# Head pairs in sparse and dilated attention, sums of 128 columns, and head gains folded into tables and copies

## The reference, cut to what matters

```python
# hybrid layer: native sparse attention, 4 heads of 64, for each of 4 blocks of 128 rows
kc, vc = compress_blocks(k, ...), compress_blocks(v, ...)        # 31 compressed keys
o_cmp = softmax(q kc^T/8 - slope*dist, causal) @ vc
o_sel = softmax over the selected blocks (all 8 blocks here, causal) @ v_s
o_win = softmax over the last 256 positions @ v_w
o = g0*o_cmp + g1*o_sel + g2*o_win

# conditioned layer l = 0, 1
qa, ka = rope(rms_norm(qa, gain_a[0])), rope(rms_norm(ka, gain_a[1]))   # 16 heads of 64 each
oa = diff_attention(qa, ka, va, lam)                                    # full 512 x 512
qb, kb = rope(rms_norm(qb, gain_b[0])), rope(rms_norm(kb, gain_b[1]))   # 12 heads of 64 each
# dilated windows (128,1), (512,4), (2048,16), 4 heads each, joined by their log-sum-exp
def rms_norm(x, g): return x * rsqrt(mean(x*x, -1) + EPS) * g
def apply_rope(x, cos, sin):            # rotates elements 0..7 with 8..15 of each 64
    x1, x2, rest = x[..., :8], x[..., 8:16], x[..., 16:]
    return concat([x1*cos - x2*sin, x2*cos + x1*sin, rest])
```

## Time and profile before

| | us |
|---|---|
| median of 3 runs | 3395.01 (3390.1 to 3413.55) |
| the profiled execution | 3409.53 |
| its span | 3407.3 |
| TensorE busy in it | 2996.8 (88%) |
| mean granted clock of TensorE | 0.872 |

### The profile page before, as it was taken

One profiled execution on the slowest core, in us unless ns is written; L12 is line 12 of the kernel. 1 busy time (PEld: TensorE's weight loads), 2 busy tenths in 40 slices (PEclk: granted clock), 3 DMA queues, 4 the chain that ended last, 5 costly groups with the idle time before them and its releaser, 6 DMA issues. The chain is left out here.

```text
span 3407.3 us, 35905 instructions
## 1 busy us (share of the span) xinstructions
PE 2996.8 (88%) x13881; PEld 2368.2 (70%) x13881; DVE 1712.8 (50%) x3234; ACT 1032.0 (30%) x2010; POOL 19.3 (1%) x58
## 2 busy tenths in 40 slices
PE   6969468886899679989999899998998999989999
PEld 5856357776688557657777688885766777768887
DVE  4223455555666365674233466645576424344444
ACT  2213221111422243543332322224354333332221
POOL 0000100000000000000000000000000000000000
PEclk8975567777899879989589899998998959999999
DMA  3210000000666202102023255521210202312221
GB/s 125 88 17 1 11 9 1 1 1 1 191 200 201 82 25 75 50 13 72 21 61 94 94 194 189 178 82 54 83 38 13 72 21 61 114 64 87 97 99 50
DMA packets 211058, 249.41 MB, mean 73 GB/s; under 512 B 12143, under 2 KB 124746, under 8 KB 210890
## 3 DMA queue, kind: packets, MB, share of 16 engines
q1 hardware_dynamic: 177056, 193.30, 17.7%
q10 hardware_dynamic: 33834, 53.83, 4.8%
HBM read 243.70 MB, written 2.10 MB: 72 GB/s over the span
## 5 line engine op out<-in xcount | busy, mean ns | idle before, releaser
L1863 ACT ACTIVATE weights_hi<-weight_ring 128x512 fp32r<-128x512 f32 (+1 forms) x240 | 143.9, 602 | 436.4 <-PE bank L1904 408.5
L1880 DVE TENSOR_TENSOR weights_lo<-weight_ring,weights_hi 128x512 fp32r<-128x512 f32 (+1 forms) x240 | 156.2, 654 | 235.6 <-ACT weights_hi L1863 235.6
L1904 PE MATMUL bank<-h_hi,weights_hi 128*128 128x512 f32 x512 | 209.7, 410 | 15.8 <-DVE h_lo L1880 9.5
L2676 PE MATMUL bank<-h_hi,weights_hi 128*128 128x512 f32 x512 | 204.0, 398 | 19.4 <-DVE h_lo L340 19.4
L789 PE MATMUL bank<-arena 64*128 64x512 f32 (+4 forms) x544 | 205.1, 614 | 17.4 <-PEq L972 11.0
L2596 ACT ACTIVATE weights_hi<-weight_ring 128x1024 fp32r<-128x1024 f32 x128 | 135.2, 1056 | 265.4 <-PE bank L2676 264.6
L2163 PE MATMUL bank<-chunk_hi,h_hi 128*128 128x512 f32 x448 | 185.5, 414 | 30.4 <-DVE h_lo L340 26.0
L1904 PE MATMUL bank<-h_lo,weights_hi 128*128 128x512 f32 x512 | 203.9, 398 | 0.0
L2676 PE MATMUL bank<-h_lo,weights_hi 128*128 128x512 f32 x512 | 203.8, 398 | 0.0
L2676 PE MATMUL bank<-h_hi,weights_lo 128*128 128x512 f32 x512 | 202.0, 395 | 0.0
L1904 PE MATMUL bank<-h_hi,weights_lo 128*128 128x512 f32 x512 | 201.8, 394 | 0.0
(11 more groups left out here) (442 smaller groups left out, 5892.8 us busy)
## 6 DMA issues: line engine op xcount, KB each, us to landing
arena<-in_ada_w ACTq DMA_DIRECT2D x48, 1024.0 KB, 5.4
weight_ring<-in_w_in SPq DMA_DIRECT2D x21, 2048.0 KB, 7.7
weight_ring<-in_w_in SPq DMA_DIRECT2D x65, 512.0 KB, 5.3
weight_ring<-in_w_mlp_up SPq DMA_DIRECT2D x16, 2048.0 KB, 8.2
weight_ring<-in_w_mlp_down SPq DMA_DIRECT2D x16, 2048.0 KB, 8.1
weight_ring<-in_w_out SPq DMA_DIRECT2D x6, 2048.0 KB, 7.9
weight_ring<-in_w_in SPq DMA_DIRECT2D x10, 1024.0 KB, 6.8
weight_ring<-in_w_branch_a SPq DMA_DIRECT2D x16, 512.0 KB, 6.4
```

Of the source, the lines that this page charges most:

```text
L1863: act.activation(hi, src, ACT.Copy).then_inc(*hi_done.one())
L1880: dve.tensor_tensor(lo, src, hi.bitcast(F32), ALU.subtract).then_inc(*lo_done.one())
L1904: ins = pe.matmul(out, ws[a_][:, n % PIECES, k - k0, :], tile["x"][b_][:, k, :], start=k + a_ + b_ == 0, stop=last[n] and k == k1 - 1 and ...
L2676: ins = pe.matmul(self.bank[t % NB][:], ws[a_][:, t % 2, k, :], x[b_][:, k, :], start=k + a_ + b_ == 0, stop=k == ND - 1 and a_ == 1)
```

## The change

1. In `attention` with one part in a unit (`nsa`, `dil`), TensorE takes the units by twos: the scores of two heads, then the transposes of the two before them, then the sums of the two before those. The row buffers are four, not three; `finish` runs six steps late, not four.
2. A sum in these stages has 128 columns of values, its head's 64 and the next 64. The columns too many are overwritten by the next head's sum. The last head of a `dil` group and the sums over compressed values stay at 64.
3. In `queries_keys` the product with the head gain is gone. For the 16 rotated elements of a head the gain is in tables of cos*gain and sin*gain; for the others it is a scale by row in ScalarE's copy from the bank, one copy for each of the four blocks. The four products of 64 columns become two of 128 (four of 64 in the chunk with queries and keys).
4. `layer_tables` loads the gains by row as well (8 more small loads of 64 rows x 2) and makes the tables (16 products of 64 columns, two memsets, two small products).

```diff
@@ attention
-        NROW = 3 * parts
+        by_twos = parts == 1
+        NROW = 4 if by_twos else 3 * parts
@@ tensor
+                def scores_of_two(n):
+                    two = units[n]["parts"] + units[n + 1]["parts"]
+                    if n >= S_BANKS:
+                        pe.wait_ge(*sig.maxima.at(n - S_BANKS + 2))
+                    lo, last = 0, len(two[0]["scores"]) - 1
+                    for j in range(last + 1):
+                        m = two[0]["scores"][j][1].shape[-1]
+                        for q, part in enumerate(two):
+                            lhsT, rhs = part["scores"][j]
+                            ins = pe.matmul(self.bank[(n + q) % S_BANKS][:, lo:lo + m], lhsT, rhs, start=True, stop=True)
+                            if j == last:
+                                ins.then_inc(*sig.scores.one())
+                        lo += m
-                steps((0, scores), (2, turn), (3, sums))
+                if by_twos:
+                    for n in range(0, N + 4, 2):
+                        if n < N:
+                            scores_of_two(n)
+                        for lag, run in ((2, turn), (4, sums)):
+                            if 0 <= n - lag < N:
+                                run(n - lag, units[n - lag])
+                                run(n - lag + 1, units[n - lag + 1])
+                else:
+                    steps((0, scores), (2, turn), (3, sums))
@@ vector
-                steps((0, maxima), (1, mix), (4, finish))
+                steps((0, maxima), (1, mix), (6 if by_twos else 4, finish))
@@ sparse_attention
-                        values = [self.ns[:, b, vcol:vcol + E] for b in range(b0, i + 1)]
+                        values = [self.ns[:, b, vcol:vcol + 2 * E] for b in range(b0, i + 1)]
@@ dilated
-                units.append(dict(parts=[part], group=2 * i, cols=(h * E, (h + 1) * E),
-                                  values=[vn[:, b, h * E:(h + 1) * E] for b in range(b0, b1)]))
+                more = E if h < H - 1 else 0
+                units.append(dict(parts=[part], group=2 * i, cols=(h * E, (h + 1) * E + more),
+                                  values=[vn[:, b, h * E:(h + 1) * E + more] for b in range(b0, b1)]))
@@ layer_tables, scalar
+                for l in range(2):
+                    for kind, name in enumerate(("qk_gain_a_2", "qk_gain_b_2")):
+                        for half in range(2):
+                            act.dma_start(self.row_gain[half * E:(half + 1) * E, l, kind, :],
+                                          a[name][l].rearrange("a e -> e a"), allow_slow_non_contiguous=True)\
+                               .then_inc(*landed.dma())
@@ layer_tables, vector
-                dve.wait_ge(*landed.all_of_stage(16 * 9))
+                dve.wait_ge(*landed.all_of_stage(16 * 17))
+                for l in range(2):
+                    for kind, gains in enumerate((self.gain_a, self.gain_b)):
+                        for j in range(2):
+                            tables = self.turns[:, l, kind, j, :].rearrange("p (i t a r) -> p i t a r", i=NT, t=2, a=2)
+                            by = gains[:, l, j, 0:2 * R].rearrange("p (a r) -> p a r", a=2).unsqueeze(1)\
+                                .broadcast_to([P, NT, 2, R])
+                            for t, angle in enumerate((self.cos, self.sin)):
+                                dve.tensor_tensor(tables[:, :, t], angle.unsqueeze(2).broadcast_to([P, NT, 2, R]), by,
+                                                  ALU.mult).then_inc(*self.dve_order.one())
@@ queries_keys, scalar
-                    act.activation(out, src, ACT.Copy).then_inc(*emptied.one())
+                    for j, which in enumerate(chunks[c][1]):
+                        to, from_ = out[:, j], src[:, j]
...
+                        ins = act.activation(to, from_, ACT.Identity, scale=self.row_gain[:, l, kind, which:which + 1])
@@ queries_keys, vector
-                    seq(tt(halves, halves, gains.unsqueeze(2).broadcast_to(shape), ALU.mult))
...
-                    for t, u, v in ((t1, x1, cos), (t2, x2, sin), (t3, x2, cos), (t4, x1, sin)):
-                        tt(t, u, v, ALU.mult).then_inc(*self.dve_order.one())
+                    for first in range(0, G, G // halves):
...
+                        for t, dst in enumerate((by_cos, by_sin)):
+                            tt(dst[:, gs], pairs[:, gs], tables[:, t].unsqueeze(1).broadcast_to([P, G // halves, 2, R]),
+                               ALU.mult).then_inc(*self.dve_order.one())
```

More of the change, by code:

```diff
@@ L755, in attention @@
         row_max = self.row_max
-        NROW = 3 * parts
+        by_twos = parts == 1
+        assert not by_twos or N % 2 == 0
+        NROW = 4 if by_twos else 3 * parts
         rows = self.take(NROW, T)
@@ L1027, in sparse_attention @@
                         part = dict(scores=[(qs[h], keys)], n=nk, table=table)
-                        values = [self.ns[:, b, vcol:vcol + E] for b in range(b0, i + 1)]
-                    units.append(dict(parts=[part], values=values, cols=(h * E, (h + 1) * E), group=g))
+                        values = [self.ns[:, b, vcol:vcol + 2 * E] for b in range(b0, i + 1)]
+                    units.append(dict(parts=[part], values=values, group=g,
+                                      cols=(h * E, h * E + values[0].shape[-1])))
                     if kind == 0:
@@ L2002, in layer_tables @@
         self.gain_a, self.gain_b = self.take(2, 2, E), self.take(2, 2, E)
+        self.turns = self.take(2, 2, 2, NT * 4 * R)
+        self.row_gain = self.take(2, 2, 2)
         self.subln = self.take(2, P)
@@ L2092, in _ @@
                     seq(ts_(self.gain_a[:, l, 0, :], self.gain_a[:, l, 0, :], E ** -0.5, None, ALU.mult))
+                    seq(ts_(self.row_gain[:, l, 0, 0:1], self.row_gain[:, l, 0, 0:1], E ** -0.5, None, ALU.mult))
                     seq(ts_(self.subln[:, l, :], self.subln[:, l, :], 1.0 - LAM[l], None, ALU.mult))
+                for half in range(2):
+                    dve.memset(self.row_gain[half * E:half * E + 2 * R], 1.0).then_inc(*self.dve_order.one())
+                dve.wait_ge(*self.act_ready.after("sin"))
+                for l in range(2):
[7 more added lines that the diff above has]
+                                                  ALU.mult).then_inc(*self.dve_order.one())
+                dve.wait_ge(*self.dve_order.all())
                 dve.wait_ge(*self.pool_ready.after("places"))
@@ L2131, in queries_keys @@
         R = E // 4 // 2
-        raw, sq = self.take(3, width), self.take(2, width)
+        raw, sq = self.take(3, width), self.obT
         ss = self.take(3, G)
-        t1, t2, t3, t4 = (self.take(G, R) for _ in range(4))
+        by_cos, by_sin = (self.take(G, 2, R) for _ in range(2))
         units = [(c, i) for c in range(len(chunks)) for i in range(NT)]
@@ L2202, in empty @@
                     src = self.bank[4 + n % 2][:, 0:width].rearrange("p (j t) -> p j t", j=NC_)
-                    if len(out.shape) == 4:
-                        src = src.rearrange("p j (b m) -> p j b m", b=NT)
-                    act.activation(out, src, ACT.Copy).then_inc(*emptied.one())
+                    for j, which in enumerate(chunks[c][1]):
+                        to, from_ = out[:, j], src[:, j]
+                        if len(to.shape) == 3:
+                            from_ = from_.rearrange("p (b m) -> p b m", b=NT)
+                        ins = act.activation(to, from_, ACT.Identity, scale=self.row_gain[:, l, kind, which:which + 1])
+                        if j < NC_ - 1:
+                            ins.then_inc(*self.x_landed.one())
+                    ins.then_inc(*emptied.one())
                 def split(n, c, i):
@@ L2232, in scale @@
                     seq(tt(x, x, ss[:, n % 3, :].unsqueeze(2).broadcast_to([P, G, E]), ALU.mult))
[L2233 to L2241 removed]
+                    pairs = x[:, :, 0:2 * R].rearrange("p g (a r) -> p g a r", a=2)
+                    halves = len(set(chunks[c][1]))
+                    for first in range(0, G, G // halves):
+                        gs = slice(first, first + G // halves)
+                        tables = self.turns[:, l, kind, chunks[c][1][first * E // P], :]\
+                            .rearrange("p (i t a r) -> p i t a r", i=NT, t=2, a=2)[:, i]
+                        for t, dst in enumerate((by_cos, by_sin)):
+                            tt(dst[:, gs], pairs[:, gs], tables[:, t].unsqueeze(1).broadcast_to([P, G // halves, 2, R]),
+                               ALU.mult).then_inc(*self.dve_order.one())
                     dve.wait_ge(*self.dve_order.all())
[L2243 removed]
+                    tt(pairs[:, :, 0, :], by_cos[:, :, 0, :], by_sin[:, :, 1, :], ALU.subtract)\
+                        .then_inc(*self.dve_order.one())
                     dve.wait_ge(*self.dve_order.all())
[L2245 removed]
+                    tt(pairs[:, :, 1, :], by_cos[:, :, 1, :], by_sin[:, :, 0, :], ALU.add).then_inc(*normed.one())
```

(8 more changed lines are left out.)

21 lines of the change are left out of this document (4 added, 17 removed).

## The result

The kernel after takes 3262.74 us (median of 4 runs, 3258.2 to 3270.46), the kernel before, beside it, 3396.56 (3390.1 to 3413.55): a ratio of 0.960, 95% interval 0.957 to 0.963. The forecast was 3268. The two profiled executions are 3409.53 and 3262.91 us long, 146.6 apart; the medians are 133.8 apart, since the profiled execution of before lies above its median.

What follows compares the result with a forecast made beforehand. TensorE, busy 88% of the span, was taken as the bound, at half clock in nsa and dil. Savings of 45 + 41 + 42 + 6.4 - 7 = 127.4 us gave 3395 - 127 = 3268, range 3240 to 3290.

Steps and rivals of the forecast that it cites:

- (a): Rival: clock stays at 1.2 GHz for its own reason, leaving only the paired scores' 65 us: 3331 us, chance 0.07.
- (b): Rival: clock stays low because transposes do not count as busy work: 3331 us, chance 0.05.
- (e): Rival: the halves do not run at once for two heads and the clock stays: 3396 us, chance 0.04.
- (d): Rival: slower, rounds run one behind the other because the second exponential is too late: 3459 us, chance 0.04.
- (c): Rival: clock rises late or falls back, above all in nsa, giving half its gain: 3300 us, chance 0.14.
- Stage by stage: Attention stages at full clock: dil 45 us instead of 86.4 and 87.0, nsa 72 instead of 117.5.
- the 12 us for the start at half clock: In nsa: it starts at half clock and its first twelve units hardly raise it, about 12 us more.
- the clock's paragraph: In nsa and both dil: rounds resembling the work before two earlier clock rises would lift the clock from about half.
- change 2's step: Sums of 128 columns in nsa and dil: cost taken as zero, at most 55 us; no gain except through the clock.
- The far rounds: Dil rounds of two far units: 2.2 us of TensorE; may lose 0.3 us each to ScalarE's queue, 7 us in all.
- Tables: Table stage: eight more loads delay VectorE's start by 3.9 us, plus products; 7 us more taken, loads' bounds 0 to 8.
- Head norms: The qk stages: middle hidden behind gapless TensorE projection, only the end shorter, 1.6 us in each of four, 6.4 saved.

Runs made afterwards that it cites:

- e6: The kernel after with 40 unused transposes in the table stage ahead of nsa: 3264.44 us against 3397.77 for the kernel before.
- x1: The kernel before with eleven unused transposes in dil's third and fourth step, where TensorE waits: 3333.3 us against 3394.06.
- x3: The kernel after with unused transposes in nsa's table stage, first two rounds and ahead of the first sixteen units' sums: 3261.0 us against 3394.06 before.
- e2: The kernel before with only the sums widened to 128 columns, one head at a time: 3363.48 us against 3408.62.
- e1: The kernel after with sums of 64 columns again, pairs of scores kept: 3287.87 us against 3408.62 for the kernel before.
- x8: The kernel after with sums of 64 columns and eleven unused transposes in dil's second and third round: 3274.94 us against 3399.37 before.
- x4: The kernel after with eleven unused transposes in dil's second and third round: 3265.15 us against 3394.06 for the kernel before.
- e7: The kernel after with ScalarE by twos, two exponentials and then two copies: 3263.52 us against 3397.77 for the kernel before.
- x5: The kernel after with the unused transposes of x3 and x4 and ScalarE's order of e7: 3257.8 us against 3394.06 for the kernel before.
- x7: The kernel before with x1's unused transposes in dil and more in nsa and its table stage: 3306.27 us against 3399.37.

## Why the prediction was right

**TensorE bounds the three stages; the clock rises.** Right: 0.96 and 1.00 in dil, and 1.00 in nsa from its 27th us on. Rivals (a), (b) and (e) fall with it, and (d) too: no round runs one behind the other. (c) had part of it, the late rise in nsa, but not its price. The rule behind (b), that the full clock does not engage for transposes, is in "TensorE: Matmul & The Clock Gate" of the Trainium skill, Part 4. The runs disagree: a transposes-only stretch at 1.00 (e6) and a stage that eleven transposes saved (x1).

**Stage by stage.** dil: 45 predicted, 43.9 and 42.6 measured; 41 and 42 saved predicted, 43.0 and 44.3 measured. nsa: 45 predicted, 48.8 measured. Of its terms, the 12 us for the start at half clock were too high: x3 takes it away and gains 1.5, at most 8.5 with the time of its own transposes taken off.

**What the clock's paragraph got wrong.** Its conclusion held and its reason only in part, so that it was partly luck. It compared what TensorE did before the two rises with dil0, and took the rounds of 64 rows and narrow sums as work under which the clock is low. It missed that 0.53 in the earlier trace rows is not 0.50: each dil stage began at full clock and lost it after about 5 us (0.03 x 2 x 87). The old rounds hold the clock for a whole stage when that wait is filled (x1: 52.5 us). What is poor in them is that they do not win it back, and neither do one-head rounds with wide sums (e2, 81.9 us). The change did nothing against the loss, which came again in the kernel after's dil0; its rounds win the clock back, which the paragraph did say. So change 2's step, no gain except through the clock, was right, and its size is 7 us in dil0, 14 in nsa and 5 in the stages behind dil (e1), against a cost of 0.5 us a stage at full clock (x8 against x4), where zero was taken. At half clock no cost can be told (e2).

**Change 1.** Alone at half clock I had given it 20 us a dil stage. At full clock it is worth 10.2 (x1 against x8), half. At half clock no stage was run that prices it; a pair of 384 columns in e1's dil0 takes 1599.55 - 1597.97 = 1.58 us, no more than one head's 1.57.

**The far rounds.** 2.30 us where 2.2 was said; ScalarE's queue costs 0.3 us in a stage at most, not 7 in two (e7). Leaving it to the range was right.

**Tables.** +7 predicted, +5.0 to +5.6 measured. The timeline of the kernel after, ScalarE's last loads and VectorE's first instruction:

```profile
1141.85 1.28 ACTq L2077 DMA_DIRECT2D arena<-in_qk_gain_b  x2
...
1144.88 0.17 DVE L2105 CAST arena<-positions 128x4 f32<-128x4 int32 x1 [11.56 <-DMA arena<-in_qk_gain_b]
```

VectorE starts 1144.88 - 1134.77 = 10.1 us into the stage, 1191.47 - 1183.42 = 8.05 before: 2.1 later, not 3.9. The scattered loads are dearer to issue (0.65 us each, not 0.48), but VectorE follows the last of them by 1.75 us, where it came 5.0 behind the last issue in the earlier trace rows: most of the issuing lies in the landing time of an earlier load. The products cost what was said: the other 2.9 of the 5.0 us, small ones included.

**Head norms.** 6.4 predicted, 10.5 measured. The end of qk_a in the kernel after, timeline:

```profile
1283.82 0.69 DVE L2292 TENSOR_TENSOR arena<-arena 128x512 f32<-128x512 f32 x1
...
1284.54 0.50 DVE L2301 TENSOR_TENSOR arena<-arena 128x128 f32<-128x128 f32 x2
...
1285.47 0.69 DVE L2292 TENSOR_TENSOR arena<-arena 128x512 f32<-128x512 f32 x1
...
1288.42 1.14 ACT L2262 ACTIVATE arena<-bank,arena 128x128 f32<-128x128 f32 x4 [0.51 <-PE bank L2229]
```

Two units are 1285.47 - 1283.82 = 1.65 us apart; in the kernel before they were 2.51. That is 0.86 a unit (0.91 said), 1.7 for two; the last copy of 0.60 has become 1.14, not 0.8, so the end gains 1.2 us a stage where 1.6 was said: 4.7 of the 10.5. What was wrong is "inside qk TensorE projects without a gap". In the kernel before, TensorE's weight loads for the turns waited for VectorE's last addition, 3.6 us in 12 times during layer 0's qk_a. In the kernel after no such wait is listed there, and the projections of that stage span 96.8 us instead of 98.7. The other 5.8 us of the four stages came from this middle, where I had counted nothing; that the shorter list is what took the wait away is the reading that fits, and no run tries it alone. A part may be the clock's, which was 0.90 in layer 0's qk_a and 0.92 in its qk_b before, and 0.92 and 0.94 after.

**Not counted.** The stage behind dil takes 9.3 us instead of 12.0, twice, with no line of it changed: it now starts at full clock. That is the 5.4 us left over. A full clock in dil was not enough for it (x1, and e1's dil1); behind wide sums it came each time.

So the single terms missed by 4 (nsa), 2 and 2 (dil), 4 (head norms), 2 (tables) and 5 us (the stages behind dil), all the same way: 147 by stages instead of 127.4. The medians are 133.8 apart, so that against them the forecast is 5 us off. That it came so near is thus luck in part: by stages it was 20 short. Executions of one kernel differ by such amounts outside the change: the recurrence stage, its code the same in all kernels, took 405 to 424 us in the profiles, with the granted clock between 0.73 and 0.78.

## What to carry to other kernels

When a stage stands on TensorE, look at the granted clock in its first microseconds, not only at its mean: a mean just over one half can be a full clock that was lost at the seam. A handful of unused transposes in that wait is a cheap trial and tells what the clock is worth before any rewriting (here 34 of 87 us a stage). Where such transposes do not stand in a wait they cost their own time, twice as much at half clock (x5). Pairing 64-row products on the two halves saves half of their own time at either clock. Making the sums wider than needed cost next to nothing here and paid only through the clock: where it had been lost, in nsa's thin units and at the seam behind the stage.

## What the runs showed of the hardware

- The same instructions ran a stage in 88.7 us at 0.54 and in 53.2 at 1.00 in one execution (e2), by what the clock was behind the stage's first microseconds. Half clock held there through 81.9 us in which TensorE was never idle.
- The level is carried over a stage's seam, but not always: full in the first 2 us of dil in all 14 kernels, while in the stage behind dil it stayed full behind wide sums and mostly fell behind narrow ones, also where dil had ended at full clock (x1, e1's dil1).
- Transposes alone raise it (e6, and the earlier trace rows). In e6, x5 and x7 the clock was 0.50 again after 4.5 to 4.6 us without TensorE work ahead of nsa, in x3 still 1.00 after 2.98.
- A sum matmul with 64 or 128 columns costs the same at half clock, 0.23 us, its weight load.
- A copy from the bank in four pieces of 128 columns costs 1.14 us, in one of 512 0.60.
